# Sums of weight blocks by accumulating DMAs in a seven-product (Strassen-like) feed-forward

## The reference, cut to what matters

```python
def swiglu(h, wg, wu, wd):
    return (jax.nn.silu(h @ wg) * (h @ wu)) @ wd

# second_block, for each layer l of 2
h = modulated_norm(x, norm_g[l, 0], sh1, sc1)
x = x + 0.5 * g1 * swiglu(h, ffn_wg[l, 0], ffn_wu[l, 0], ffn_wd[l, 0])
...                                    # attention and pooling, or a short convolution
h = modulated_norm(x, norm_g[l, 2], sh3, sc3)
x = x + 0.5 * g3 * swiglu(h, ffn_wg[l, 1], ffn_wu[l, 1], ffn_wd[l, 1])
```

## Time and profile before

| | us |
|---|---|
| median of 3 runs | 2662.86 (2662.83 to 2662.94) |
| the profiled execution | 2662.88 |
| its span, first to last instruction | 2661.1 |
| TensorE busy in the span | 2645.2 |
| VectorE busy | 1757.9 |
| ScalarE busy | 1086.7 |
| GpSimd busy | 71.2 |

### The profile page before, as it was taken

One profiled execution on the slowest core, in us unless ns is written; L12 is line 12 of the kernel. 1 busy time (PEld: TensorE's weight loads), 2 busy tenths in 40 slices (PEclk: granted clock), 3 DMA queues, 4 the chain that ended last, 5 costly groups with the idle time before them and its releaser, 6 DMA issues.

```text
span 2661.1 us, 37114 instructions
## 1 busy us (share of the span) xinstructions
PE 2645.2 (99%) x14953; PEld 2314.2 (87%) x14953; DVE 1757.9 (66%) x2177; ACT 1086.7 (41%) x1497; POOL 71.2 (3%) x119
## 2 busy tenths in 40 slices
PE   8999999999999999999999999999999999999999
PEld 7888988888888888888878999989899988898998
...
GB/s 145 64 63 63 79 97 95 184 199 204 201 201 188 144 202 201 202 197 143 95 48 85 106 95 111 82 93 111 96 111 105 101 83 102 84 112 93 114 95 80
DMA packets 257929, 324.33 MB, mean 122 GB/s; under 512 B 5766, under 2 KB 248708, under 8 KB 249604
## 3 DMA queue, kind: packets, MB, share of 16 engines
...
## 4 chain that ended last, share of the span: by engine, by line
PE 99%; ACT 0%; DVE 0%; DMA 0%; issue 0%; DVEq 0%; ACTq 0%
PE po L749 18%; PE po L750 18%; PE po L751 18%; PE po L1122 6%; PE po L1123 6%; PE po L1124 6%; PE po L919 2%; PE po L921 2%; PE po L920 2%; PE pm L950 1%; PE po L818 1%; PE po L820 1%; PE po L833 1%; PE po L852 1%; PE po L861 1%; PE po L866 1%
## 5 line engine op out<-in xcount | busy, mean ns | idle before, releaser
L1505 ACT ACTIVATE w_hi<-w_raw 128x1024 fp32r<-128x1024 f32 x326 | 329.6, 1050 | 567.6 <-PE po L751 529.6
L2285 DVE TENSOR_TENSOR w_lo<-w_raw,w_hi 128x1024 fp32r<-128x1024 f32 x364 | 432.8, 1221 | 176.1 <-ACT w_hi L1505 170.7
L749 PE MATMUL po<-b_hi,w_hi 128*128 128x512 f32 x1008 | 393.2, 390 | 0.0
L750 PE MATMUL po<-b_lo,w_hi 128*128 128x512 f32 x1008 | 392.7, 390 | 0.0
L751 PE MATMUL po<-b_hi,w_lo 128*128 128x512 f32 x1008 | 392.7, 390 | 0.0
L749 PE MATMUL po<-a_hi,w_hi 128*128 128x512 f32 x976 | 380.5, 390 | 0.0
L751 PE MATMUL po<-a_hi,w_lo 128*128 128x512 f32 x976 | 380.2, 390 | 0.0
L750 PE MATMUL po<-a_lo,w_hi 128*128 128x512 f32 x976 | 380.1, 389 | 0.0
L751 PEld LDWEIGHTS po<-b_hi,w_lo 128*128 128x128 f32 x1008 | 189.3, 188 | 39.4
L750 PEld LDWEIGHTS po<-b_lo,w_hi 128*128 128x128 f32 x1008 | 189.4, 188 | 38.7
L749 PEld LDWEIGHTS po<-b_hi,w_hi 128*128 128x128 f32 x1008 | 189.4, 188 | 38.7
...
## 6 DMA issues: line engine op xcount, KB each, us to landing
ada_in<-in_w_ada_dram POOLq DMA_DIRECT2D x64, 1152.0 KB, 5.5
w_raw<-in_ffn_wg_dram SPq DMA_DIRECT2D x44, 1024.0 KB, 5.4
w_raw<-in_ffn_wu_dram SPq DMA_DIRECT2D x44, 1024.0 KB, 5.4
w_raw<-in_w_ff_dram SPq DMA_DIRECT2D x32, 1024.0 KB, 5.2
w_raw<-in_ffn_wd_dram SPq DMA_DIRECT2D x32, 1024.0 KB, 5.0
w_raw<-in_w_in_dram SPq DMA_DIRECT2D x27, 1024.0 KB, 5.0
...
w_raw<-in_w_in_c_dram SPq DMA_DIRECT2D x12, 1024.0 KB, 5.1
```

The source lines that it names most:

```text
L749: pe.matmul(o, wh, hi[:, k, :], start=(k == ks[0]), stop=False)
L750: pe.matmul(o, wh, lo[:, k, :], start=False, stop=False)
L1505: act.activation(w_hi[:, s, part], w_raw[:, s, part], ACT.Copy).then_inc(hi_done, 1)
L2285: dve.tensor_tensor(w_lo[:, s, part], w_raw[:, s, part], w_hi[:, s, part].bitcast(F32), ALU.subtract).then_inc(lo_done, 1)
```

## The change

Of the four sums for each of gate and up, two are no longer made by VectorE. With other signs, sum 1 is upper right + lower right and sum 3 is upper left + upper right, both plain additions of a block of the same weight matrix; so each is an accumulating DMA from HBM onto the quarter that lies in `w_raw`, issued from GpSimd's queue (`add_blocks`), four per pair, 256 KB each. Sum 2 becomes sum 3 + lower right, sum 4 lower left + sum 2. ScalarE's batches 4 and 5 wait for both DMAs of their matrix, VectorE's sum 2 for that of the left column. The signs of the token sums and of the reads of the results (u3, silu21, c22, mul21) are changed to match. Nothing is changed on TensorE and SyncE.

```diff
@@ -353,6 +353,8 @@
         s_x_sum = sem("block_sums_dve")
+        lower_added = [sem("lower_row_added_gate"), sem("lower_row_added_up")]
+        column_added = [sem("left_column_added_gate"), sem("left_column_added_up")]
         s_y_act, s_y_dve, s_y_pe = sem("seven_act"), sem("seven_dve"), sem("seven_pe")
...
@@ -446,11 +448,11 @@
         x_dve = [Steps(s_x_dve[b], ["lo"], reps=n_seven) for b in range(5)]
-        x_sum = Steps(s_x_sum, [f"s{m}{c}" for c in "gu" for m in (3, 2, 4, 1)], reps=n_seven)
+        x_sum = Steps(s_x_sum, ["s2g", "s4g", "s2u", "s4u"], reps=n_seven)
         y_act = Steps(s_y_act, ["u1g", "u1u", "u2g", "u2u", "u3g", "u3u", "silu21", "silu22", "silu1"], reps=n_seven)
...
         y_pe = Steps(s_y_pe, ["p1g", "p2g", "p1u", "p2u", "p6g", "p6u", "p7g", "p7u", "p4g", "p4u"], reps=n_seven)
-        t_dve = Steps(s_t_dve, ["step", "r1", "r3", "r2", "r4", "lo2", "lo3", "lo4", "lo1"], reps=len(SEVEN))
+        t_dve = Steps(s_t_dve, ["step", "minus", "r1", "r3", "r2", "r4", "lo2", "lo3", "lo4", "lo1"], reps=len(SEVEN))
         t_act = Steps(s_t_act, ["hi2", "hi3", "hi4", "hi1"], reps=len(SEVEN))
...
@@ -721,6 +723,27 @@
+            def add_blocks(l, j, g, i):
+                ug = U_FFN[l, j, g] + 2 * i
+                w = SEVEN_FIRST[l, j, g] + i
+                r0 = sum(GROUPS[:g]) * P + i * PAN
+                for s, weight in enumerate((ffn_wg_2, ffn_wu_2)):
+                    blocks = weight[l, j].rearrange("(k p) n -> p k n", p=P)[:, :, r0 + P:r0 + PAN]
+                    pool.wait_ge(raw_landed[s], 8 * ug + 16)
+                    pool.dma_start(raw_block(s, 1, 0), blocks[:, 4:8, :], accum_op=ALU.add)\
+                        .then_inc(lower_added[s], 16)
+                for s, weight in enumerate((ffn_wg_2, ffn_wu_2)):
+                    blocks = weight[l, j].rearrange("(k p) n -> p k n", p=P)[:, :, r0 + P:r0 + PAN]
+                    pool.wait_ge(s_x_dve[s], x_dve[s].after("lo", w))
+                    pool.dma_start(raw_block(s, 0, 0), blocks[:, 0:4, :], accum_op=ALU.add)\
+                        .then_inc(column_added[s], 16)
+            for l, j in SEVEN:
+                for g, n in enumerate(GROUPS):
+                    for i in range(seven_from(l, j, g), n // 2):
+                        add_blocks(l, j, g, i)
         @block.tensor
...
@@ -1903,8 +1926,11 @@
                     act.wait_ge(raw_landed[batch - 1], 8 * ug + 16)
+                elif batch in (4, 5):
+                    act.wait_ge(lower_added[batch - 4], 16 * (w + 1))
+                    act.wait_ge(column_added[batch - 4], 16 * (w + 1))
                 else:
-                    act.wait_ge(s_x_sum, x_sum.after({3: "s2u", 4: "s1g", 5: "s1u", 6: "s4g", 7: "s4u"}[batch], w))
+                    act.wait_ge(s_x_sum, x_sum.after({3: "s2u", 6: "s4g", 7: "s4u"}[batch], w))
                 if head:
...
@@ -1920,10 +1946,9 @@
                 e = SEVEN.index((l, j))
-                shift = norm_cols(f"{l}{2 * j}")[1]
                 act.wait_ge(s_t_dve, t_dve.after("r4", e))
                 for k in range(4):
-                    ins = act.activation(t_hi[:, 0, k, :], t_raw[:, 0, k, :], ACT.Identity, bias=shift[:, 4 + k:5 + k])
+                    ins = act.activation(t_hi[:, 0, k, :], t_raw[:, 0, k, :], ACT.Identity, bias=small[:, 44 + k:45 + k])
                 ins.then_inc(s_t_act, t_act.one("hi2"))
...
@@ -1953,7 +1978,8 @@
                     act.wait_ge(s_y_pe, y_pe.after(after, w))
-                    act.activation(ev[:, 1, q * QT:(q + 1) * QT], first_bank(s), ACT.Copy)\
+                    act.activation(ev[:, 1, q * QT:(q + 1) * QT], first_bank(s), ACT.Copy,
+                                   scale=-1.0 if step[:2] == "u3" else 1.0)\
                         .then_inc(s_y_act, y_act.one(step))
...
@@ -1987,7 +2013,8 @@
                 act.wait_ge(s_y_pe, y_pe.after("p4g", w))
-                act.activation(ev[:, 0, 2 * QT:3 * QT], first_bank(0), ACT.Silu).then_inc(s_y_act, y_act.one("silu21"))
+                act.activation(ev[:, 0, 2 * QT:3 * QT], first_bank(0), ACT.Silu, scale=-1.0)\
+                    .then_inc(s_y_act, y_act.one("silu21"))
                 if head:
...
@@ -2920,19 +2947,13 @@
                 s = "gu".index(c)
-                if step[:2] == "s3":
-                    dve.wait_ge(s_x_dve[s], x_dve[s].after("lo", w))
-                    out_, a, b, op = raw_block(s, 0, 0), raw_block(s, 0, 0), raw_block(s, 1, 0), ALU.subtract
-                elif step[:2] == "s2":
-                    dve.wait_ge(s_x_sum, x_sum.after("s3" + c, w))
-                    out_, a, b, op = sum_block(s), raw_block(s, 1, 1), raw_block(s, 0, 0), ALU.subtract
-                elif step[:2] == "s4":
+                if step[:2] == "s2":
+                    dve.wait_ge(column_added[s], 16 * (w + 1))
+                    out_, a, b = sum_block(s), raw_block(s, 0, 0), raw_block(s, 1, 1)
+                else:
                     dve.wait_ge(s_x_sum, x_sum.after("s2" + c, w))
-                    out_, a, b, op = raw_block(s, 0, 1), raw_block(s, 0, 1), sum_block(s), ALU.subtract
-                else:
-                    dve.wait_ge(s_x_sum, x_sum.after("s3" + c, w))
-                    out_, a, b, op = raw_block(s, 1, 0), raw_block(s, 1, 0), raw_block(s, 1, 1), ALU.add
-                dve.tensor_tensor(out_, a, b, op).then_inc(s_x_sum, x_sum.one(step))
+                    out_, a, b = raw_block(s, 0, 1), raw_block(s, 0, 1), sum_block(s)
+                dve.tensor_tensor(out_, a, b, ALU.add).then_inc(s_x_sum, x_sum.one(step))
...
@@ -2940,6 +2961,8 @@
                     .then_inc(s_t_dve, t_dve.one("step"))
+                dve.tensor_scalar(small[:, 44:48], shift[:, 4:8], -1.0, None, ALU.mult)\
+                    .then_inc(s_t_dve, t_dve.one("minus"))
                 dve.wait_ge(s_n_dve, norm_dve[f"{l}{2 * j}"].after(f"t{DK - 1}b"))
...
@@ -2947,26 +2970,30 @@
+                def less(step, out_, a, b):
+                    for m in range(2):
+                        ins = dve.scalar_tensor_tensor(out_(m), a(m), -1.0, b(m), ALU.mult, ALU.subtract)
+                    ins.then_inc(s_t_dve, t_dve.one(step))
                 def summed(buf):
...
-                both("r1", summed(t1_raw), rows_of(0, 1), rows_of(0, 0), ALU.subtract)
+                both("r1", summed(t1_raw), rows_of(0, 0), rows_of(0, 1), ALU.subtract)
                 both("r3", summed(t_raw[:, 1]), rows_of(2, 1), rows_of(0, 1), ALU.subtract)
                 dve.wait_ge(s_t_dve, t_dve.after("r3", e))
-                both("r2", summed(t_raw[:, 0]), summed(t_raw[:, 1]), rows_of(0, 0), ALU.add)
+                less("r2", summed(t_raw[:, 0]), summed(t_raw[:, 1]), rows_of(0, 0))
                 dve.wait_ge(s_t_dve, t_dve.after("r2", e))
-                both("r4", summed(t_raw[:, 2]), rows_of(2, 0), summed(t_raw[:, 0]), ALU.subtract)
+                less("r4", summed(t_raw[:, 2]), summed(t_raw[:, 0]), rows_of(2, 0))
...
                 e = SEVEN.index((l, j))
-                shift = norm_cols(f"{l}{2 * j}")[1]
                 dve.wait_ge(s_t_act, t_act.after("hi2", e))
                 for k in range(4):
-                    ins = dve.scalar_tensor_tensor(t_lo[:, 0, k, :], t_raw[:, 0, k, :], shift[:, 4 + k:5 + k],
+                    ins = dve.scalar_tensor_tensor(t_lo[:, 0, k, :], t_raw[:, 0, k, :], small[:, 44 + k:45 + k],
                                                    t_hi[:, 0, k, :].bitcast(F32), ALU.add, ALU.subtract)
...
@@ -3016,7 +3043,7 @@
                     dve.wait_ge(s_y_act, y_act.after("u3" + c, w))
-                    dve.tensor_tensor(out_, ev[:, 1, (2 * s + 1) * QT:(2 * s + 2) * QT], other_bank(s), ALU.add)\
+                    dve.tensor_tensor(out_, ev[:, 1, (2 * s + 1) * QT:(2 * s + 2) * QT], other_bank(s), ALU.subtract)\
                         .then_inc(s_y_dve, y_dve.one("c22" + c))
...
@@ -3041,12 +3068,9 @@
                 lo(1)
-                total("s3g")
                 total("s2g")
                 total("s4g")
-                total("s1g")
                 lo(2)
-                total("s3u")
                 if head:
...
@@ -3055,7 +3079,6 @@
                     fourth_block("u", hid[:, 3 * QT:4 * QT])
-                total("s1u")
                 if not more:
...
@@ -3070,8 +3093,8 @@
                 dve.wait_ge(s_y_act, y_act.after("silu21", w))
-                dve.tensor_tensor(hid[:, 2 * QT:3 * QT], ev[:, 0, 2 * QT:3 * QT], first_bank(1), ALU.mult)\
-                    .then_inc(s_y_dve, y_dve.one("mul21"))
+                dve.scalar_tensor_tensor(hid[:, 2 * QT:3 * QT], first_bank(1), -1.0, ev[:, 0, 2 * QT:3 * QT],
+                                         ALU.mult, ALU.mult).then_inc(s_y_dve, y_dve.one("mul21"))
                 dve.wait_ge(s_y_act, y_act.after("silu22", w))
...
@@ -3101,26 +3124,21 @@
                 block_lo(2, l, j, 0, i)
-                for step in ("s3g", "s2g", "s4g", "s1g", "s3u", "s2u"):
```

(6 more changed lines are left out.)

## The result

| | before | after |
|---|---|---|
| time, median | 2662.9 (2662.83 to 2663.21, 4 runs) | 2892.06 (2890.41 to 2897.03, 4 runs) |
| span of the profiled execution | 2661.1 | 2895.2 |
| TensorE busy in the span | 2645.2 | 2708.5 |
| VectorE busy | 1757.9 | 1690.4 |
| GpSimd busy | 71.2 | 210.7 |

What follows compares the result with a forecast made beforehand. TensorE was taken to bound the kernel, with 15.9 us idle. Stalls of 11Du + 6Dc - 26.4 = 47.6 us per feed-forward, 143 in three, gave 2806 us; the range was 2730 to 2890.

Steps and rivals of the forecast that it cites:

- What bounds the kernel: Whole program: TensorE busy 2645.2 of 2661.1 us; the sums taken from VectorE are worth 0 to the span.
- Two round trips in a row behind the up load: Per pair, on VectorE's order: two DMA round trips one after the other, the first beginning when the up load landed.
- Du: Time from the end of low part 2 to the landing of up's left-column DMA: 4.0 us, 2.5 to 5.5.
- Dc: Time from the landing of the up load to that of gate's left-column DMA: 5.0 us, 3.0 to 7.
- (a): Pair behind a pair that isn't its group's first: stall Dc + Du - 2.3 = 6.7 us, one per feed-forward.
- (b): Pair behind a group's first pair: stall Dc + Du - 0.6 = 8.4 us, two per feed-forward.
- (c): First pair of the second and third group: stall 3Du + Dc - 7.7 = 9.3 us, two per feed-forward.
- (d): Opening pair of the first group: stall 2Du + Dc - 7.5 = 5.5 us.
- Rivals 1 and 2: 1: both DMAs fit in the slack, 2663 us, 3%; 2: DMAs near the plain copy, 2720 to 2755, 14%.
- Rival 3: Accumulating DMAs near or over the upper end, since each engine must read what it adds to: 2860 to 2950, 16%.
- Rival 4: TensorE's clock falls to 1.2 GHz at stops in 18 of 27 pairs: 26 us, 2831, or 2885; 13%.
- The sign posts: VectorE's sum 2 waits twice per pair; TensorE waits 6 to 9 us at its twelfth or fourteenth product in 18 pairs.

Runs made afterwards that it cites:

- the shorter DMAs above: Changed kernel with accumulating DMAs of 128 KB (2825.1 us), or with plain copies, sums left out, from GpSimd's queue (2816.1) or SyncE's (2775.4).
- the filled stalls: Changed kernel with idle block products, into a bank that nothing reads, put where TensorE waits: 2890.95 us.
- The plain copies: Changed kernel with its four DMAs as plain copies, sums left out: 2816.1 us from GpSimd's queue, 2775.4 from SyncE's.

## Why the prediction was wrong in size and right in kind

Direction, mechanism and places held; the time, 2892, lies 2 us above the range, and 86 above the forecast. In turn:

- **What bounds the kernel: right.** Nothing was won by taking 67 us off VectorE.
- **Two round trips in a row behind the up load: right.** VectorE waits for a DMA in 53 of 54 sums 2, and the shorter DMAs above move the time about as the sum says.
- **Du, 4.0, measured 5.0: the first failed term.** Its parts were 2.5 for the plain copy (2.9 from SyncE), 0.8 for the adding (1.2), 0.7 for GpSimd's descriptors (0.5), and nothing for the ways between: from low part 2's end to the issue 0.3, from the landing to sum 2 0.1 to 0.25. Three of these small things lengthen it, one shortens it.
- **Dc, 5.0, measured 6.6: the second.** I allowed 0.53 us for the issue of lower up. It takes 1.28, column gate behind it 1.86, and column gate lands 5.7 us after its row's start. I blamed the rows per partition in advance; the larger part is the adding, since a plain issue with the same rows takes 0.75.
 Together these make 11 x 1.0 + 6 x 1.6 = 20.6 us per feed-forward, 62 in all.
- **The sum by places.** From the distance of one read (first up block) to the next in both traces, averaged over the three feed-forwards; these are the profiled executions, so three feed-forwards make the 234 us:

| place | predicted | with measured Du, Dc | measured |
|---|---|---|---|
| (a) | 6.7 | 9.3 | 10.5 |
| (b) | 8.4 | 11.0 | 11.6 |
| (c) | 9.3 | 13.9 | 15.8 |
| (d) | 5.5 | 9.1 | 12.6 |
| feed-forward | 47.6 | 68 | 78 |

 **The third failed term is a place left out.** In (d) 2.3 us lie ahead of the opening pair's first read (1.8, 3.1 and 1.9), since the product of the last plain pair (`hid L3161`) stands behind the opening blocks with their two waits; TensorE itself begins that pair some 1.1 us late. I counted only what comes after. **The fourth is the clock, put at nothing:** of the 30 us by which three feed-forwards exceed the sum with measured Du and Dc, it has some 13 by the filled stalls. The two don't strictly add up, since a stop takes in what was late ahead of it, and the rest stays open; the largest excess is that of (c), the pairs with two stops.
- **Rivals 1 and 2 did not come.** The plain copies show what rival 2 would have been: 2816 from GpSimd, 2775 from SyncE, above its 2720 to 2755 even for a copy.
- **Rival 3 is nearest to what happened**, in its range of 2860 to 2950, with durations near its ends (5.0 of 5.5, 6.6 of 7), though not for its reason alone: adding is 1.2 of 4.6 us.
- **Rival 4: its fact right, its price about half.** The clock fell to 0.50 behind every stop of 1.9 us and more; those of up to 1.6 us left it at 1.00. The Trainium skill (TensorE: Matmul & The Clock Gate, Part 1) says that an idle TensorE falls to 1.2 GHz; the trace agrees (0.50 after 2063.5). The 26 us of this rival were to come from the product between the read and the release of the next load. That way shows in one place only, the up load of (a), up to 1.3 us later; the 13 us found above come from slow matmuls that no stall follows.
- **The chances.** Rivals 3 and 4 were set as alternatives to the forecast with one fault each. Nothing excludes long durations and a slow clock in the same run, and here both came; the range should have gone on from the upper ends (2891) with the 26 us of the clock, to 2917.
- **The sign posts** held in part. VectorE waits twice per pair and its busy time fell, by 67 us and not 74; the DMAs land 4.6 us after their issue, not 4. TensorE's waits at the twelfth product are 3.5 to 10.1 us long, not 6 to 9, and there are others: six of up to 4.7 us at the third product of a group, which the sum has in (c), and three for `hid L3161`, which it hasn't. And one sign of being wrong came: the clock row fell below 1.

The plain copy of 256 KB on GpSimd's queue, in pieces of 512 bytes, took 3.4 us from issue to landing. The Trainium skill (DMA: Bandwidth & Descriptors, Anatomy of one DMA) gives 2.0 us and bytes over 436 GB/s for a DMA on this queue; by it 256 KB would take 2.6 us, an estimate. The measurement decides. My parts without the adding came to 3.2, nearer, and not long enough either.
